# Token-major projections: both halves of a weight chunk in one 512-column matmul per token tile

## The reference, cut to what matters

```python
h = rms_norm(x, norm_mix) * (1 + sc_m) + sh_m
(aq, ak, ..., cqkv, cz, ca, cb) = jnp.split(h @ w_in, points, axis=-1)
o_a = banded_attention(...)
o_b = nsa_mixer(...)
o_c = gated_delta_net(cqkv, ca, cb, cz, conv_w, A_log, dt_bias, gdn_norm)
x = x + gt_m * (jnp.concatenate([o_a, o_b, o_c], axis=-1) @ w_out)
...
o = moba_attention(q, k, v, table_hk)                         # even layer, half of the heads
out = dsa_attention(q, k, v, q_idx, k_idx, w_idx, table_hk)   # even layer, the others
o = dilated_mixture(q, k, v, table_hk)                        # odd layer
```

## Time and profile before

| | |
|---|---|
| median of 3 runs | 1587.56 us (1587.52 to 1589.96) |
| span of the profiled execution | 1582.1 us |
| TensorE busy | 1491.2 us, 94% of the span |
| VectorE busy | 1010.9 us, 64% |
| ScalarE busy | 811.6 us, 51% |
| GpSimd busy | 294.3 us, 19% |
| HBM traffic over the span | 185 GB/s |

### The profile page before, as it was taken

How to read it: one execution, slowest core, us unless ns; L and a number is a source line. 1 busy time by engine, 2 the same in 40 slices (tenths; PEclk the granted TensorE clock), 3 DMA queues, 4 the chain that set the end, 5 groups by cost and what they waited for, 6 DMA issues and landing times.

```text
span 1582.1 us, 29674 instructions
## 1 busy us (share of the span) xinstructions
PE 1491.2 (94%) x12380; PEld 1419.4 (90%) x12380; DVE 1010.9 (64%) x1342; ACT 811.6 (51%) x1319; POOL 294.3 (19%) x190
## 2 busy tenths in 40 slices
PE   6999988999989999889999998979999999899997
PEld 2997878999889877889999997879999998899997
DVE  1685457876657844576546577657885655677854
ACT  3774365443347544544434455456754456566642
POOL 0002203997900022058000001100000001000000
PEclk8999999999999999999999999989999999999999
DMA  9455665764544365165535542244535543344442
GB/s 387 167 198 214 224 207 213 256 257 182 227 169 180 122 260 213 55 237 189 190 141 192 213 161 107 107 160 160 199 140 183 200 157 140 128 160 165 174 155 92
DMA packets 31925, 287.92 MB, mean 182 GB/s; under 512 B 3079, under 2 KB 11559, under 8 KB 12488
## 3 DMA queue, kind: packets, MB, share of 16 engines
q1 hardware_dynamic: 27400, 267.42, 45.6%
q0 software_dynamic: 2304, 16.78, 2.9%
q10 hardware_dynamic: 2112, 2.15, 0.4%
HBM read 285.23 MB, written 7.39 MB: 185 GB/s over the span
## 4 chain that ended last, share of the span: by engine, by line
PE 80%; DVE 8%; ACT 7%; issue 3%; POOL 1%; DMA 1%; SPq 0%; DVEq 0%; ACTq 0%
PE bank L656 23%; PE bank L657 22%; PE bank L658 22%; DVE w_lo L1964 2%; ACT w_hi L1448 2%; PE bank L969 1%; PE bank L800 1%; PE bank L759 1%; PE bank L952 1%; PE bank L967 1%; PE bank L813 1%; PE bank L773 1%; PE bank L735 1%; PE bank L788 1%; DMA ring<-ada 1%
## 5 line engine op out<-in xcount | busy, mean ns | idle before, releaser
L656 PE MATMUL bank<-hi_T,w_hi 128*128 128x256 f32 x2184 | 630.6, 289 | 30.4 <-DVE h_lo L1949 17.0
L658 PE MATMUL bank<-hi_T,w_lo 128*128 128x256 f32 x2184 | 624.7, 286 | 0.0
L1964 DVE TENSOR_TENSOR w_lo<-ring,w_hi 128x2048 fp32r<-128x2048 f32 (+1 forms) x226 | 508.3, 2256 | 180.5 <-ACT w_hi L1448 178.7
L657 PE MATMUL bank<-h_lo,w_hi 128*128 128x256 f32 x2056 | 588.8, 286 | 0.0
L1448 ACT ACTIVATE w_hi<-ring 128x2048 fp32r<-128x2048 f32 (+1 forms) x226 | 391.7, 1734 | 262.9 <-PE bank L658 242.7
L656 PEld LDWEIGHTS bank<-hi_T,w_hi 128*128 128x128 f32 x2184 | 426.6, 195 | 36.6 <-issue 30.0
L658 PEld LDWEIGHTS bank<-hi_T,w_lo 128*128 128x128 f32 x2184 | 426.3, 195 | 0.0
L657 PEld LDWEIGHTS bank<-h_lo,w_hi 128*128 128x128 f32 x2056 | 402.2, 196 | 0.4 <-issue 0.2
L656 PE MATMUL bank<-act_hi,w_hi 128*128 128x256 f32 x704 | 200.0, 284 | 5.7 <-DVE w_lo L1964 5.7
L657 PE MATMUL bank<-act_lo,w_hi 128*128 128x256 f32 x704 | 199.2, 283 | 0.0
L658 PE MATMUL bank<-act_hi,w_lo 128*128 128x256 f32 x704 | 199.2, 283 | 0.0
(11 more groups left out here) (268 smaller groups left out, 1923.9 us busy)
## 6 DMA issues: line engine op xcount, KB each, us to landing
ring<-w_gu SPq DMA_DIRECT2D x22, 2048.0 KB, 7.8
ring<-w_dn SPq DMA_DIRECT2D x32, 1408.0 KB, 6.1
ring<-w_up SPq DMA_DIRECT2D x22, 2048.0 KB, 7.9
ring<-ada SPq DMA_DIRECT2D x16, 2048.0 KB, 9.0
ring<-w_mix SPq DMA_DIRECT2D x11, 2048.0 KB, 8.2
arena<-ada POOLq DMA_DIRECT2D x16, 1024.0 KB, 6.8
ring<-even_in SPq DMA_DIRECT2D x8, 2048.0 KB, 7.8
ring<-odd_in SPq DMA_DIRECT2D x6, 2048.0 KB, 7.9
```

The costliest lines, as they stand in the source:

```text
L656: nc.tensor.matmul(out, wh, xh, start=start, stop=False)
L657: nc.tensor.matmul(out, wh, xl, start=False, stop=False)
L658: return nc.tensor.matmul(out, wl, xh, start=False, stop=stop)
L1964: V.tensor_tensor(w_lo[:, n % SLOTS, at], ring[:, n % SLOTS, at], w_hi[:, u % AHEAD, 0:size].bitcast(F32), ALU.subtract).then_inc(w_lo_rea ...
```

## The change

The token-major chunks move both weight halves in one matmul. `side_by_side` makes one operand of 2 x 256 columns from two halves' places in `w_hi` (or `w_lo`), and `wide_token_tile` makes one token tile with 24 matmuls of 512 columns. It waits for the second half at its start. Both halves come free when the second token tile is done (`KINDS`). `log_decays` stands between the two tiles. On ScalarE `tokens_taken` takes one tile at a time, and the two `high` of the following halves stand behind the second. On VectorE the `low` move accordingly. The diff without repeated or trivial hunks:

```diff
-    KINDS = dict(columns=((2, 4), (1, 2, 3, 4)), tokens=((1, 3), (2, 3)), rows=((1, 3), (2, 3)),
+    KINDS = dict(columns=((2, 4), (1, 2, 3, 4)), tokens=((2, 2), (1, 2)), rows=((1, 3), (2, 3)),
                  down=((1, 2), (2,)), tail=((1, 4), (2, 3, 4)), compress=((), ()))
...
                         channel_tile(bank[:, (first_bank + t) % 4, 0:S], w, m * P, src).then_inc(gemm_ready, 1)
 
-            def tokens_chunk(name, nn, j, first_bank=0, parts=(0, 1)):
-
-                for part in parts:
-                    u = phases[name]["u0"] + 2 * nn + part
-                    half_in(u)
-                    w = split_half(u, CH // 2)
-                    for qt in range(QT):
-                        if part == 0:
-                            tile_free(name, j + qt)
-                        last = token_tile(bank[:, (first_bank + j + qt) % 4, CH // 2 * part:CH // 2 * (part + 1)], w, 0, CH // 2,
-                                          (hi_T, h_lo), qt)
-                        if part == 1 or qt == QT - 1:
-                            last.then_inc(gemm_ready, 1)
+            def side_by_side(a, b):
+
+                return bass.AP(tensor=a.tensor, offset=a.offset,
+                               ap=[list(a.ap[0]), [b.offset - a.offset, 2], list(a.ap[1])])
+
+            def wide_token_tile(out, u, qt):
+
+                half_in(u + 1)
+                (ah, al), (bh, bl) = split_half(u, CH // 2), split_half(u + 1, CH // 2)
+                qs = slice(qt * P, qt * P + P)
+                for k in range(KT):
+                    hi, lo = side_by_side(ah[:, k, :], bh[:, k, :]), side_by_side(al[:, k, :], bl[:, k, :])
+                    last = three(out, (hi_T[:, k, qs], h_lo[:, k, qs]), (hi, lo), k == 0, k == KT - 1)
+                last.then_inc(gemm_ready, 1)
 
...
                 rotate(l, 5)
-                tokens_chunk(name, 2, 8, 2, parts=(0,))
-                log_decays(l)
-                tokens_chunk(name, 2, 8, 2, parts=(1,))
+                for qt in range(QT):
+                    tile_free(name, 8 + qt)
+                    wide_token_tile(bank[:, 2 + qt, :], phases[name]["u0"] + 4, qt)
+                    if qt == 0:
+                        log_decays(l)
 
             def mixing(l):
...
                         channel_tile(bank[:, WOVEN[(j + m) % 3], 0:S], w, m * P, (hi_T, h_lo)).then_inc(gemm_ready, 1)
 
-                def tokens_half(i, j):
-                    part = i % 2
-                    half_in(h0 + i)
-                    w = split_half(h0 + i, CH // 2)
-                    for qt in range(QT):
-                        if part == 0:
-                            taken(j + qt - 2)
-                        last = token_tile(bank[:, WOVEN[(j + qt) % 3], CH // 2 * part:CH // 2 * (part + 1)], w, 0, CH // 2,
-                                          (hi_T, h_lo), qt)
-                        if part == 1 or qt == QT - 1:
-                            last.then_inc(gemm_ready, 1)
-
-                return taken, columns_half, tokens_half
+                def token_tile_of(i, j, qt):
+                    taken(j + qt - 2)
+                    wide_token_tile(bank[:, WOVEN[(j + qt) % 3], :], h0 + i, qt)
+
+                return taken, columns_half, token_tile_of
...
                 index_scores(2)
                 index_scores(3)
-                tokens_half(8, 15)
+                token_tile_of(8, 15, 0)
                 index_scores(4)
                 index_scores(5)
-                tokens_half(9, 15)
+                token_tile_of(8, 15, 1)
                 index_scores(6)
...
                 values(u0 + 1)
                 transposes(u0 + 2)
-                tokens_half(14, 25)
+                token_tile_of(14, 25, 0)
                 values(u0 + 2)
                 transposes(u0 + 3)
                 taken(25)
                 pe.wait_ge(k_scaled, 4)
                 scores(u0 + 4)
-                tokens_half(15, 25)
+                token_tile_of(14, 25, 1)
                 values(u0 + 3)
                 scores(u0 + 5)
...
-                taken, columns_half, tokens_half = woven_halves(ph["t0"], ph["u0"])
+                taken, columns_half, token_tile_of = woven_halves(ph["t0"], ph["u0"])
 
                 half_in(ph["u0"])
                 first_tiles(split_half(ph["u0"], CH // 2), (hi_T, h_lo), normalised(first))
                 sum_late_squares(1)
                 columns_half(1, 2)
-                tokens_half(2, 4)
+                token_tile_of(2, 4, 0)
                 turn_rows(1)
                 taken(4)
                 pe.wait_ge(k_scaled, 6)
                 scores(u0)
-                tokens_half(3, 4)
...
                 scores(u0 + 5)
-                tokens_half(10, 18)
+                token_tile_of(10, 18, 0)
                 values(u0 + 3)
                 transposes(u0 + 4)
                 taken(18)
                 pe.wait_ge(k_scaled, 9)
                 scores(u0 + 6)
-                tokens_half(11, 18)
+                token_tile_of(10, 18, 1)
...
                     take(name, j + m, qk2[:, t, :], bank[:, WOVEN[(first + j + m) % 3], 0:S])
                 high(at + AHEAD)
 
-            def tokens_taken(name, j, at, first, half):
-
-                for qt in range(QT):
-                    act.wait_ge(gemm_ready, phases[name]["tile_event"][j + qt])
-                    nc.scalar.activation(vv2[:, qt, CH * half:CH * half + CH], bank[:, WOVEN[(first + j + qt) % 3], :],
-                                         ACT.Copy, scale=r_column[:, qt:qt + 1]).then_inc(gemm_freed, 1)
-                high(at + AHEAD)
+            def tokens_taken(name, j, first, half, qt):
+
+                act.wait_ge(gemm_ready, phases[name]["tile_event"][j + qt])
+                nc.scalar.activation(vv2[:, qt, CH * half:CH * half + CH], bank[:, WOVEN[(first + j + qt) % 3], :],
+                                     ACT.Copy, scale=r_column[:, qt:qt + 1]).then_inc(gemm_freed, 1)
 
             def index_relu(i):
 
...
                 index_relu(2)
                 index_relu(3)
-                high(h0 + 8 + AHEAD)
+                tokens_taken("even", 8, 7, 0, 0)
                 index_relu(4)
                 index_relu(5)
-                tokens_taken("even", 8, h0 + 9, 7, 0)
+                tokens_taken("even", 8, 7, 0, 1)
+                high(h0 + 8 + AHEAD)
                 index_relu(6)
                 index_relu(7)
+                high(h0 + 9 + AHEAD)
                 columns(10, 10, (2, 3))
                 exps(u0)
                 columns(12, 11, (6, 7))
...
                 columns(16, 13, (12, 13))
                 exps(u0 + 3)
                 copy_pt(u0 + 2)
-                high(h0 + 14 + AHEAD)
+                tokens_taken("even", 18, 7, 1, 0)
                 copy_pt(u0 + 3)
                 exps(u0 + 4)
-                tokens_taken("even", 18, h0 + 15, 7, 1)
+                tokens_taken("even", 18, 7, 1, 1)
+                high(h0 + 14 + AHEAD)
                 exps(u0 + 5)
+                high(h0 + 15 + AHEAD)
                 mix_high_woven(slice(0, 4), u0 + 4)
                 columns(20, 16, (10, 11))
                 copy_pt(u0 + 4)
...
                 columns(0, 0, 0)
                 late_root(1)
                 columns(2, 1, 2)
+                act.wait_ge(column_ready, 2)
+                for qt in range(QT):
+                    tokens_taken("odd", 4, 0, 0, qt)
                 high(h0 + 2 + AHEAD)
-                act.wait_ge(column_ready, 2)
-                tokens_taken("odd", 4, h0 + 3, 0, 0)
+                high(h0 + 3 + AHEAD)
                 exps(u0)
                 columns(6, 4, 4)
                 copy_pt(u0)
...
                 columns(16, 9, 14)
                 copy_pt(u0 + 3)
                 exps(u0 + 4)
-                high(h0 + 10 + AHEAD)
+                tokens_taken("odd", 18, 0, 1, 0)
                 copy_pt(u0 + 4)
                 exps(u0 + 5)
                 mix_high_woven(slice(0, 4), u0 + 4)
-                tokens_taken("odd", 18, h0 + 11, 0, 1)
+                tokens_taken("odd", 18, 0, 1, 1)
+                high(h0 + 10 + AHEAD)
+                high(h0 + 11 + AHEAD)
                 copy_pt(u0 + 5)
                 exps(u0 + 6)
                 exps(u0 + 7)
...
                 low(h0 + 7 + AHEAD)
                 index_sums(2)
                 index_sums(3)
-                low(h0 + 8 + AHEAD)
                 index_sums(4)
                 index_sums(5)
                 scale_keys(4, "even", 8)
-                low(h0 + 9 + AHEAD)
+                low(h0 + 8 + AHEAD)
                 index_sums(6)
                 index_sums(7)
+                low(h0 + 9 + AHEAD)
                 dve.wait_ge(bias_in, 16)
                 logits(u0)
                 highest(0, 0, 4)
...
                 highest(1, 4, 6)
                 recip(u0 + 3)
                 scale_keys(12, "even", 18)
-                low(h0 + 14 + AHEAD)
                 highest(1, 6, 8)
                 evac(u0 + 2)
```

(9 more changed lines are left out.)

3 lines of the change are left out of this document (2 added, 1 removed).

## The result

The changed kernel takes 1603.1 us (median, 1600.2 to 1604.2) against 1587.5 us before: the ratio of the runs is 1.0103, with a 95% interval of 1.0091 to 1.0115. It is some 16 us slower. A second measurement of the same kernel, beside other runs of before, gave 1.0103 again (1.0088 to 1.0119). The forecast was 10.4 us slower, 1598.0.

What follows compares the result with a forecast made beforehand. TensorE, busy 94% of the span, was taken to bound the kernel. Terms of 2.46 + 1.57 + 1.6 + 1.6 + 1.15 = 8.4 us, 10.4 with the clock, on 1587.56 gave 1598.0 us, range 1590.0 to 1603.5.

Steps and rivals of the forecast that it cites:

- Part 3: Four woven chunks: two splits fall due at one point, a late split costs +1.57, +1.6, +1.6 and +1.15 us.
- Part 4: First odd chunk: TensorE's wait grows from 1.54 to about 3.8 us, the granted clock falls to 0.50, +2.0 us.
- Part 1: Token tiles: 288 matmuls of 512 columns at 0.2267 us against 0.240 for a pair, 3.8 us saved over six chunks.
- 0.240: Rival on token tiles: a wide matmul costs two narrow ones, nothing saved, 1601.8 us; 0.15 together with a worse second even chunk.
- as cheap as a narrow one: Rival on token tiles: a wide matmul takes a narrow one's 0.120 us, about 1567 us; chance 0.02.
- Part 2: Two hybrid chunks: TensorE waits 1.87 us for VectorE's low part, less 0.64 saved, +1.23 each, +2.46 us for both.
- Part 3, even chunks, 3.17: Even woven chunks: late logits +1.57 us at the first, a late mix low +1.6 us at the second.
- Part 3 and 4, first odd chunk, 3.6: First odd chunk: two low parts ahead of the logits, +1.6 us, and half the clock behind TensorE's wait, +2.0 us.
- Part 3, second odd chunk, 1.15: Second odd chunk: VectorE's copy of values comes late behind two lows, TensorE's next values start 1.15 us later.
- The clock did not stay up: Rival at the first odd chunk: the granted clock stays up, the 2.0 us fall away, 1596.0 us; chance 0.20.
- the splits were not hidden: Rival at the four woven chunks: late splits hidden, -3.5 us there, 1586.5 us in all, not slower; chance 0.12.

## Why the prediction was right or wrong, point by point

- **The step that failed.** Two terms of the sum, which together were too small. Part 3 put +1.6 us on the first odd chunk; without the clock its trace shows 3.8 us (the shift goes from 7.75 to 11.54), because POOL's product took 3.19 us beside a low part and not 1.04. And Part 4 priced half the clock at that one place, with 2.0 us (measured 2.3 there); it also followed the wait at the second odd chunk (1.5 us, beside a term of 1.67 instead of 1.15), and in some executions the waits of the hybrid chunks (1.6 us each). Over the five rows of the table the two executions have 15.2 and 18.0 us against 10.4 forecast.
- **Sign and place.** Right: the two splits that fall due at one point are the cause. With the same waits and narrow matmuls the loss is 19.8 us. With the low part ahead of the rotations the loss goes at the hybrid places, and with the reciprocal first at the first odd one.
- **Part 1, the wide matmul, 0.2267 us.** Right to the third digit. The 3.8 us saved were measured as 3.5, give or take 3, in the times and as some 2 at the places in the traces. The two rivals that priced it otherwise (0.240, or as cheap as a narrow one) are out.
- **Part 2, the hybrid chunks, 2.46.** Measured 2.66 where the clock stayed up. The term left out that this wait, too, can be followed by half the clock: of four traces with this order and wide tiles it followed at both places in two (5.9 us together), at one in one, at none in one.
- **Part 3, even chunks, 3.17.** Measured 3.2 and 2.9, right in the sum by luck. At the second one the delay did not come through the mix low (1.21 us, it escaped POOL as assumed), but through ScalarE's queue: second high, mix copy, then the copy that frees TensorE's bank. I had that high ahead of the mix copy in the sum and did not ask who waits for what stands behind it. The wait was 2.72 us, with a halved clock behind it; with that high behind the copies it was 0.92. Alone, the first chunk's growth was 0.4 us (1.57 forecast) and the second's 2.3 (1.6).
- **Part 3 and 4, first odd chunk, 3.6.** Measured 6.1: 3.8 and, for the clock, 2.3. The term mis-sized is the 1.6: it took POOL's product at the 1.04 us that it had while VectorE was idle. In the change the next half's high is ready early, so its low part starts right behind the reciprocal and takes the product from 1.04 to 3.19. The same doubling of a price stood in the earlier trace rows (a low part of the mix at 2.28 us beside POOL, 1.20 alone); I used it on VectorE's side and not on POOL's. Moving that low part by one line gave 3.2 us back over the place. With the wait then at the forecast's length, the place cost 2.9 us instead of 3.6: the clock then took 1.2 us in a stretch of 3.4 us, so the 2.0 of Part 4 was too high for the forecast's own wait.
- **Part 3, second odd chunk, 1.15.** Measured 3.2: the term itself 1.67, the rest a halved clock behind a wait of 2.83 us for VectorE's copy (L2022), which came late as forecast. That this clock was not priced belongs to the failed step.
- **The rivals.** The clock did not stay up, and the splits were not hidden: the waits for POOL grew from 1.40 to 3.59 us and from 1.54 to 5.91, so they are in one line with the logits. At the first even chunk most of it was absorbed all the same.
- **The frame.** The prediction laid the 5.5 us between median and span around the span. Each execution of the later kernels takes 2.1 us more than its span (1600.16 and 1598.1), so the profiled execution of before was itself some 3.4 us faster than the median. Against it, kernels that are unchanged up to 906 us are 0.3 to 5.4 us late by then. This moved no term, but the 0.8 and 1.0 us outside the places are of this kind and not of the change.
- **The range.** Its upper end of 1603.5 lies just above the measured median, and just below 1603.9, what the ratio makes of 1587.5. It lacked the cost of POOL's product and of the clock at the other places, 2.2 us and 1.5 us apiece.

## What to carry to other kernels

A larger matmul that needs two buffers at once also frees them at once: price the step that refills them, and find in each queue, ScalarE's too, who stands behind the second refill. When an engine gets work earlier, ask what it will run beside: here a VectorE instruction moved up against a POOL product tripled the product on the path. A wait that is made longer may cost another 1.5 to 2.6 us in granted clock, as it did here, and one that is taken away may not be won.

## What the runs showed of the hardware that was not expected

POOL's product of 128 x 512 takes 1.04 us alone and 2.9 to 3.2 us beside a VectorE subtraction of two SBUF operands (2.29 us alone); two such subtractions took 5.31 us beside it instead of 4.50. A matmul of 512 columns out of two pieces of 256, each from another half of the weights in `w_hi` or `w_lo`, runs at 0.227 us, the columns plus the same 0.013 us that one of 256 carries. Behind one and the same wait of TensorE, as that of 1.66 us in the hybrid layers, the granted clock was 1.00 in one execution and 0.50 in another; where it was 0.50 the place cost 1.6 us more.
